# A cap of five on the key-block loads that GpSimd has in flight in a decode step of block-sparse attention

## What is computed

```python
def _layer(x, attend, g_pre, w_in, ...):
    h = _rms(x, g_pre)
    z = jnp.einsum('btd,df->btf', h, w_in)              # 1024 -> 3584 columns
    ua, va, ga, qb, kb, vb, gb = jnp.split(z, SPLIT_AT, axis=-1)
    ya, v_rows = chunk_mlp(ua, va, sgu_gain, sgu_w, sgu_b)
    yb = attend(q, k, v)                                # 8 heads of 64
    ya = _rms(ya, g_branch_a) * jax.nn.silu(ga)
    yb = _rms(yb, g_branch_b) * jax.nn.silu(gb)
    y = jnp.einsum('btf,fd->btd', jnp.concatenate([ya, yb], axis=-1), w_out)
    return x + _rms(y, g_post), ...

def moba_sample(...):                                   # for each of the 8 samples
    k_full = cache_k[page_table].reshape(8, 16, 256, 8, 64)   # 16 blocks of 256 positions
    kmean = jnp.mean(k_full, axis=2)
    gate = jnp.einsum('bhtd,bnhd->bhtn', q, kmean)
    _, sel = lax.top_k(gate, 3)                         # three blocks for each head
    # scores of q with the keys of the chosen blocks and of the new token, minus an ALiBi
    # distance penalty; softmax; sum of the chosen blocks' values
```

## Time and profile before

| | |
|---|---|
| median of 3 runs | 524.53 us (517.46 to 530.83) |
| profiled execution | 516.84 us |
| its span, first to last instruction | 515.1 us |
| mean granted TensorE clock | 0.923 of full speed |
| busy: PE, PEld, DVE, ACT, POOL | 436.1, 192.2, 281.0, 124.9, 242.3 us |
| moved by DMA | 110.95 MB, mean 215 GB/s |

### The profile page before, as it was taken

One profiled execution on the slowest core, in us unless ns is written; L12 is line 12 of the kernel. 1 busy time (PEld: TensorE's weight loads), 2 busy tenths in 40 slices (PEclk: granted clock), 3 DMA queues, 4 the chain that ended last, 5 costly groups with the idle time before them and its releaser, 6 DMA issues.

```text
span 515.1 us, 7913 instructions
## 1 busy us (share of the span) xinstructions
PE 436.1 (85%) x2264; PEld 192.2 (37%) x2264; DVE 281.0 (55%) x749; ACT 124.9 (24%) x290; POOL 242.3 (47%) x356
## 2 busy tenths in 40 slices
PE   6989983999389985999739997799798997798993
PEld 3423431343034532555324543234333343243430
DVE  1535732366055764969445585559542674658253
ACT  2411100000123524553222544142122111000112
POOL 5875277105840054911763117862578357517111
PEclk9989997999699985999955999899999998899998
DMA  8995499545996069911998009993899169924121
GB/s 286 400 394 180 165 382 380 74 165 164 391 283 204 7 198 296 288 15 43 341 391 187 1 22 342 382 335 87 270 303 360 24 232 373 327 30 106 63 81 43
DMA packets 76698, 110.95 MB, mean 215 GB/s; under 512 B 44568, under 2 KB 45080, under 8 KB 76656
## 3 DMA queue, kind: packets, MB, share of 16 engines
q0 software_dynamic: 22576, 71.45, 39.6%
q1 hardware_dynamic: 42720, 21.14, 16.5%
q10 hardware_dynamic: 11360, 17.86, 10.3%
HBM read 106.11 MB, written 4.29 MB: 214 GB/s over the span
## 4 chain that ended last, share of the span: by engine, by line
PE 36%; DVE 14%; another core or an unknown queue 13%; DMA 12%; issue 9%; POOL 8%; ACT 2%; DVEq 2%; ACTq 1%; SPq 1%; POOLq 0%
PE PA L957 17%; DMA K<-in_cache_k,kidx 10%; POOL K L820 6%; PE PA L1047 5%; PE GB L1063 5%; DVE ksum L1492 3%; PE SB L1003 3%; PE PO L1024 2%; DMA V<-in_page_table 1%; DVE ksum L684 1%; PE SB L1012 1%; POOL rstd L834 1%; PE SB L911 1%; DVEq L1490 1%
## 5 line engine op out<-in xcount | busy, mean ns | idle before, releaser
L820 POOL DMA_INDIRECT K<-in_cache_k,kidx x128 | 128.3, 1002 | 146.3 <-DVE ksum L1492 110.8
L957 PE MATMUL PA<-wbuf,hT 128*128 128x512 f32 x384 | 189.0, 634 | 0.0
L684 DVE TENSOR_TENSOR ksum<-K 128x512 f32<-128x512 f32 x128 | 85.1, 688 | 72.3 <-DMA K<-in_cache_k,kidx 54.2
L957 PEld LDWEIGHTS PA<-wbuf,hT 128*128 128x128 f32 x384 | 72.1, 200 | 94.7 <-issue 93.6
L669 POOL DMA_DIRECT2D V<-in_cache_v x128 | 75.5, 594 | 49.9 <-issue 38.9
L1047 PE MATMUL PA<-wbuf,hT 128*128 128x512 f32 x128 | 61.6, 622 | 0.1
L1063 PE MATMUL GB<-ksum,win 128*32 128x512 f32 x256 | 39.6, 675 | 16.4 <-DVE ksum L684 12.3
L1492 DVE TENSOR_TENSOR ksum<-K,qb 128x128 f32<-128x128 f32 x192 | 42.0, 286 | 11.4 <-issue 5.9
L833 POOL TENSOR_SCALAR rstd<-msum 128x1 f32<-128x1 f32 (+3 forms) x24 | 7.9, 330 | 62.3 <-ACT junk L1136 36.6
L1047 PEld LDWEIGHTS PA<-wbuf,hT 128*128 128x128 f32 x128 | 23.3, 194 | 28.3 <-issue 27.7
L1024 PE MATMUL PO<-v,pT 128*128 128x64 f32 x160 | 23.9, 284 | 7.9 <-DVE yb L1410 7.4
(11 more groups left out here) (186 smaller groups left out, 377.7 us busy)
## 6 DMA issues: line engine op xcount, KB each, us to landing
wbuf<-in_w_in ACTq DMA_DIRECT2D x5, 2048.0 KB
V<-in_cache_v SPq DMA_DIRECT2D x240, 32.0 KB
V<-in_cache_v POOLq DMA_DIRECT2D x128, 32.0 KB, 6.3
wbuf<-in_w_out ACTq DMA_DIRECT2D x2, 2048.0 KB
wbuf<-in_w_in SPq DMA_DIRECT2D x4, 512.0 KB, 8.2
wbuf<-in_w_in SPq DMA_DIRECT2D x1, 2048.0 KB
K<-in_cache_k,kidx POOLq DMA_INDIRECT x128, 12.6
qb<-q_rows SPq DMA_DIRECT2D x8, 256.0 KB
```

Of the source, the lines that this page charges most:

```text
L684: eng.tensor_tensor(ksum[:, n % SUMS, :], K[:, n, 0, :], K[:, n, 1, :], ALU.add).then_inc(s_dsum, 1)
L820: pool.indirect_dma_start(K[:, n, :, :].rearrange("p r w -> p (r w)"), None, k_rows, bass.IndirectOffsetOnAxis(ap=kidx[:, b, n:n + 1], axis=0)
L957: last = pe.matmul(bank[:, :], lhs, rhs, start=(kc == 0), stop=(kc == KC - 1))
```

## The change

In the program, GpSimd waits before the load of block n (n from 5 to 15) until block n-5 of the same sample has landed. So at most four blocks can be on their way when it issues the next, and five after it. In the plan, the load of block n gets the landing of block n-5 as a dependency. Nothing else is edited.

```diff
@@ make_plan
     for b in range(B):
         for n in range(NB):
             deps = [("DVE", ("ex", b - 1, PARTS - 1))] if b else []
+            if n >= FLIGHT:
+                deps.append(("Q", ("k", b, n - FLIGHT)))
             add("POOL", "load", ("ld", b, n), 1.25, *deps)
             add("Q", "key", ("k", b, n), KEY_US, ("POOL", ("ld", b, n)))
@@
 TILE_US, KEY_US, LAG, MARGIN, SLACK, QUARTERS = 7.2, 1.65, 0.25, 0.3, 0.05, 4
+FLIGHT = 5
@@ block.gpsimd, kind == "ld"
                     if b >= 1 and n == 0:
                         pool.wait_ge(s_ext, b)
+                    if n >= FLIGHT:
+                        pool.wait_ge(s_k[n - FLIGHT], 16 * (b + 1))
                     load_k(NB * b + n)
```

## The result

| | before | after |
|---|---|---|
| median of 4 runs each | 523.06 us (517.46 to 530.83) | 486.86 us (482.35 to 492.37) |
| profiled execution, its span | 516.84, 515.1 us | 492.37, 490.6 us |

The ratio is 0.9285, 95% interval 0.9171 to 0.9399: **7% faster**, where 525 us and a range of 503 to 546 were forecast.

A forecast was written before the change was run, and what follows sets the result against it. PE's own work and each sample's key loop were taken to bound it. Waits and landings cost 0; 516.84 + 1.2 = 518.0 us profiled, with the median 7.7 higher 525.7, said as 525 us, range 503 to 546.

The forecast's parts named there:

- what bounds the kernel now: PE's work alternating with each sample's key loop; PE idle 32.9 us in samples 1 to 4, cause not told.
- the first rival: Key queue depth holds PE; the cap shortens idle in samples 1, 2, 4, at most 27.1 us; 503 us; chance 0.31.
- the second rival: PE is held until POOL stops issuing keys; the cap prolongs that by 20.4 us; 546 us; chance 0.28.
- the four stretches that I had cut: Time windows in key loads of samples 1 to 4; PE idle 9.1, 9.6, 5.8 and 8.4 us there.
- Does the wait bite?: POOL's key loads: nearly everywhere yes; last load 5.6 us later in sample 1, 9.4 in sample 4.
- Does a block land later?: Last key block of a sample: transfers stay busy, 0 us taken, bound 0 to 3 us from samples 5 to 7.
- the margin of 4 x 1.45 us: Four key blocks still outstanding when POOL is released, 5.8 us of transfer, keep the queue from running dry.
- Behind POOL's wait: Value DMAs, `rstd` steps and sample 0's constants queued after key loads on POOL: 0 us; `rstd` up to 3 us.
- the bound of 3: Sample 5's tile 2 `rstd` on POOL: cost 0, up to 3 us if DVE's new order asks early.
- What the plan moves: Reordered steps from sample 4's loads on: 0 us, bounds -4 to +4; program end +1.2 us.
- The seven quarters: PE projection quarters between the last value product and `fin2`: 7 x 1.91 = 13.4 us.
- The rule weighed: DMA engines take turns between queues, so SP's value rows stay as slow beside the keys; sum unchanged.

The follow-up runs named there:

- e11: The wait alone with a cap of five in samples 1, 2 and 4 only, against the kernel before; 488.84 us, ratio 0.9381.
- e1: The wait on block n-5 alone, added to the kernel before with its plan unchanged; 483.47 us against 520.88, ratio 0.9328.
- e2: The new plan dependency alone, without the wait, against the kernel before; 533.81 us, ratio 1.0198.
- e9: Kernel before plus the cap of five keys and five extra indirect loads a sample of 128 rows of 16 bytes; 556.64 us, ratio 1.0696.
- e15: Kernel before with one wait a sample: load 8 waits until block 3 has landed; 491.04 us, ratio 0.9566.
- e13: Kernel before plus the cap of five keys and five extra indirect loads a sample of 16 rows of 512 bytes; 551.07 us.
- e14: Kernel before plus the cap of five keys and five extra direct DMAs a sample of 128 rows of 16 bytes; 490.97 us, ratio 0.9541.
- e17: Kernel before without a cap, plus five extra direct DMAs a sample of 128 rows of 16 bytes; 478.17 us, ratio 0.9182.
- e18: Kernel before without a cap, plus two POOL memsets before each of key loads 2, 5, 8, 11 and 14; 479.84 us, ratio 0.9214.
- e16: Kernel before plus five extra indirect 16-row loads a sample, each indirect load waiting for the fifth before it; 514.82 us, ratio 0.9899.
- e6: Kernel before, no wait on landings, a POOL memset before each key load but the first; 480.82 us, ratio 0.9214.
- e7: Kernel before, no wait on landings, a POOL memset only before key loads 9 to 15; 521.37 us, ratio 0.9915.
- e8: Kernel before without a cap; SP's value rows wait until the sample's sixteen key blocks have landed; 531.88 us, ratio 1.0193.

## Why the prediction was wrong, point by point

**The step that failed** is the third sentence from the end of "what bounds the kernel now" and what I made of it: that nothing in the trace told what holds PE, and so that PE's idle stretches would stay as they are, 0 us. They were nearly the whole of the effect: PE's idle time in the stretches of samples 1 and 2 went from 9.1 and 9.6 us to 0 and 0.9, and the cap in samples 1, 2 and 4 alone (e11) brought 34.7 us. The effect stood there as the first rival, and I gave it 0.31 and at most 27.1 us. Its cause stood there by halves: it is POOL's indirect loads that hold PE, but the pace of their issue, which the second rival named, orders the cases better than the depth (see what stays open). What I set against the first rival was misread. Sample 3 has short loads, 6.5 us at the median, and six in flight nevertheless, and PE is busy there for 6.83, 7.52 and 9.72 us of 10 with caps of five, four and three, against 2.97 without. I had taken the landing time of its loads as a measure of how many are in flight.

**The size of the first rival.** Samples 1, 2 and 4 brought 31.5 us in e1 (27.9 between the two traces) against "at most 27.1", and 503 us, some 22 us less than no change, was my price. The bound counted idle time in three of the four stretches that I had cut; the distance from sample to sample would have been the honest bound.

**Does the wait bite?** Yes. The last load of sample 1 went out 87.00 - 61.51 = 25.5 us after the first, against 80.1 - 61.1 = 19.0: 6.5 us later, 5.6 predicted. POOL waited 39.2 us for keys in 34 places. Issue to landing is 8.2 us at the median by the view in which it was 12.6; 7 was predicted. I had read the 12.6 as the median of all loads. It is that of blocks 14 and 15, where the queue is long; by the DMA records the median of all 128 was 9.2 before and is 7.3 now.

**Does a block land later?** Yes, by more than the 0 that I took. By the semaphore, block 15 of sample 1 was issued at 87.0 and landed 7.6 us later, 33.1 us after the first issue, against 92.9 - 61.1 = 31.8. By the DMA records it is 31.3 against 28.7, and in the eight samples the last block comes 0.9 to 4.4 us later after the first issue than before: in samples 5 to 7, to which I had given 3 us in sum, 3.3, 3.9 and 1.9. In sample 1 that is small beside what was won: the block was added at once, at 95.17, where it had waited until 105.35. Now that a sum follows its landing, such a delay may reach the end; no run separates it. A cap of three shows the cliff that the margin of 4 x 1.45 us guarded: 528.95 us.

**Behind POOL's wait.** The value rows end at 100.6, 39.1 us after the first key, against 35.2: 3.9 us later, not 0. Short waits between them stayed (0.26 to 0.49 us); I had predicted none. The `rstd` of tile 2 in sample 5 (compare and the earlier trace rows), on POOL and DVE:

```profile
305.27 1.05 POOL L837 TENSOR_TENSOR rstd<-rstd,nhalf 128x4 f32<-128x4 f32 x1
```

```profile
306.35 1.14 DVE L1353 SCALAR_TENSOR_TENSOR vn<-vn,rstd,gain 128x128 f32<-128x128 f32 x4 [1.26 <-POOL rstd L837]
```

DVE waits 1.26 us for it, inside the bound of 3.

**What the plan moves.** 0 was taken, -4 to +4. e2 without the wait is 10.0 us slower between the traces (12.9 by the medians), 3.5 of them behind sample 3. Beside the cap it can't be seen: e1 without the moves 0.9328, after with them 0.9285, within each other's intervals. The end of the program on PE (compare) and the last copy on the chain:

```profile
461.03 0.86 PE L1097 MATMUL DC<-V,pex 128*32 128x64 f32 x46
461.82 3.70 PE L1052 MATMUL PA<-wbuf,hT 128*128 128x512 f32 x8
...
465.55 8.85 PE L1052 MATMUL PA<-wbuf,hT 128*128 128x512 f32 x20
474.87 0.41 PE L1111 MATMUL SB<-ident,yas 8*128 8x8 f32 x4 [0.47 <-DVE obs L1565]
475.89 1.92 PE L916 MATMUL SB<-wbuf,hTs 128*32 128x512 f32 x16 [0.36 <-issue]
```

```profile
481.34 0.59 ACT spart L1269
```

The last value product ends at 461.89, as that of before at 483.83. The seven quarters take 12.6 us, not 13.4, and `fin2` begins at 474.87, 13.0 us behind the product, the last 0.47 of them a wait for DVE. From the product's end to `spart` it is 19.5 us, and the 3.8 us of quarters in front of it make 23.3, against 23.2 predicted and 22.0 before: +1.3 where +1.2 stood.

**The second rival**, PE held until POOL stops issuing, 546 us, is dead as a price: POOL issues longer and PE works. What I had seen in it is real all the same. In most of the long cases the results come 2 to 4 us after an indirect load of POOL behind which it pauses: 3.4 in samples 1 and 4 of before with five and seven keys in flight, 3.5 in e9 with none. In sample 3 of before POOL, on its timeline, pauses behind the tenth load, and DVE, held for 8.69 us by a late result, goes on 2.3 us after that load, with six loads still to be issued:

```profile
194.74 0.94 POOL L820 DMA_INDIRECT K<-in_cache_k,kidx  x1 [0.30 <-issue]
201.86 0.49 POOL L833 TENSOR_SCALAR rstd<-msum 8x4 f32<-8x4 f32 x1 [6.18 <-ACT junk L1136]
```

```profile
197.96 0.18 DVE L1409 RECIPROCAL rinv<-ssum 128x4 f32<-128x4 f32 x1 [8.69 <-remote]
```

So PE is let go soon after a run of issues ends, with four key loads in flight here and seven in sample 4. What this rival had wrong is that issuing at a slower pace holds PE too.

**The rule weighed.** By turns between queues (the Trainium skill, "DMA: Bandwidth & Descriptors", Queues, rings and completion order) SP's rows should have stayed as slow. They took 15.63 us instead of 25.34 with the transfers as full as before, so that in this case the measurement decides against the sum drawn from it. The advice of the same page to issue a DMA early and wait late (Rules for kernel authors) also pointed the wrong way here: issuing as early as POOL can is what costs, 37 us of 521.

**What stays open.** In samples 1 and 2 the late results go with the number of indirect loads in flight: 3.1 us at most with five or fewer, 0.1 to 6.5 with six, mostly 9 to 15 with seven and eight. Against a mere count stand e15 (seven, reached late in the sample, 2.5 and 6.0 us), e9 and e13 (six with the small ones, 15 to 20 us), sample 3 (7.1 us late with five keys in e1, under 0.8 with five in e14, e17 and e18), sample 3 of e16 (five, 12.8), sample 4 of e6, e17 and e18 (eight, 3.3, 0.1 and 4.0) and samples 5 to 7 of before with five to nine and 0.7 to 5.4 us.

The pace of issue orders the samples 1 to 4 of all twenty traces better. Take the time from the start of an indirect load, small ones counted, to that of the ninth behind it, where it is shortest in the sample:

| ten indirect loads in | cases | in flight | longest late result |
|---|---|---|---|
| 10.9 to 12.0 us | 32 | 5 to 9 | 7.6 to 19.9 us |
| 12.7 us and more | 48 | 3 to 8 | 0.0 to 9.4 us, over 7 in three, all of sample 3 |

Sample 5 of before, which both rivals had against them, fits: `rstd` steps stand between its loads, ten take 13.3 us, and nothing is over 0.8 us late. Samples 0 and 7 don't keep to it: before has ten in 11.8 and 11.3 us there and results 1.9 and 5.4 us late. The order was found in the traces afterwards, ten was chosen by looking, and no run holds the pace fixed while the number in flight changes, so that it is a correlation. What in the chip passes PE's results and SP's issues on so late isn't shown by any run.

## What to carry to other kernels

When readers on several engines wait with "remote" as releaser, compare the end of the record that they need with their start: if it is many microseconds earlier, the engine that looks idle is not short of work, and the distance between loop rounds, not busy time, bounds what can be won. A long unbroken run of indirect loads on POOL is worth a cap, or a small pause, above all in its first half; try the cap on both sides, since three was 8 us slower than none and five 37 us faster. And test the count that you believe in with loads that carry next to nothing: it was those that showed that the bytes don't matter.

## What the runs showed of the hardware that was not expected

- PE's results can reach their readers 10 to 20 us late while PE itself works on, until it waits for one of those readers (12.2 us in sample 1 of before, 19.9 in e9), with the DMA engines nearly full in both cases (share 1.05 and 0.99) and in the runs without delay as well (1.05 to 1.08).
- SP's issue of a value row is slowed in the same stretches: sixteen in 25.34 us before, 15.63 with the cap, 31.41 in e9.
- Five indirect loads of 16 rows of 512 bytes in each sample beside the cap cost some 58 us of the whole (540.2 and 542.3 in the two quickest executions, against 483.47); as many direct loads of 128 rows of 16 bytes cost 7.5 (490.97).
- In the stretch from 75 to 85 us the granted clock was 0.63 to 0.80 where PE stood (before, e2, e7, e8) and 1.00 where it worked, so that a part of what the late results cost may be the lower of the two levels, 1.2 GHz, at which PE goes on. No run here separates it.
